# A two-layer decoder trunk on one core: the first column group of the input projection by row-tile halves, with its weights in a space of their own

## The reference

```python
for l in range(DEPTH):                      # 2
    a = rms_norm(h, norm_mix_pre[l])
    mix = hybrid_mixer(a, ...)              # proj = a @ w_in, three kinds of heads, then w_out
    h = h + rms_norm(mix, norm_mix_post[l])
    a = rms_norm(h, norm_x_pre[l])
    h = h + rms_norm(cross_attention(a, rms_norm(mem, norm_mem[l]), ...), norm_x_post[l])
    a = rms_norm(h, norm_ffn_pre[l])
    h = h + rms_norm(conv_ffn(a, ...), norm_ffn_post[l])
return h
```

## Time and profile before

| | |
|---|---|
| Median of three timed runs | 1779.3 us (1778.06 to 1780.26) |
| Profiled execution, its own time | 1777.65 us |
| Its span, first to last instruction | 1775.9 us |
| TensorE busy | 1714.9 us (97%) |
| ScalarE, VectorE, GpSimd busy | 714.2, 667.5, 808.5 us |
| Moved by DMA | 154.15 MB, 87 GB/s |

### The profile page before, as it was taken

The page is one execution under the profiler, slowest core; times in us unless marked ns, Lnnn a source line. Parts: engine busy times, 40 slices in busy tenths (PEclk is TensorE's granted clock), DMA queues, the critical chain, the costliest instruction groups (busy, mean ns, idle before and its releaser), DMA issues.

```text
span 1775.9 us, 23057 instructions
## 1 busy us (share of the span) xinstructions
PE 1714.9 (97%) x9214; PEld 1384.6 (78%) x9214; DVE 667.5 (38%) x1392; ACT 714.2 (40%) x1344; POOL 808.5 (46%) x495
## 2 busy tenths in 40 slices
PE   5999999999999999999989999999999999999997
PEld 4888766788688888888878886768877888888785
DVE  3253566251443223311253446651532622232113
ACT  5325657362453222232253257662633612222222
POOL 4446656364143444445344466563531344443552
PEclk9999989999999999999999999999999999999999
DMA  4324111133122222232232340111421233232321
GB/s 168 107 87 145 49 25 25 60 118 131 36 95 72 95 95 95 86 104 96 96 110 85 106 132 25 25 49 60 155 95 36 72 102 103 98 100 72 119 95 48
DMA packets 100694, 154.15 MB, mean 87 GB/s; under 512 B 4284, under 2 KB 76268, under 8 KB 100588
## 3 DMA queue, kind: packets, MB, share of 16 engines
q1 hardware_dynamic: 97532, 147.16, 25.4%
q10 hardware_dynamic: 3056, 5.51, 1.0%
HBM read 150.56 MB, written 2.10 MB: 86 GB/s over the span
## 4 chain that ended last, share of the span: by engine, by line
PE 89%; DVE 3%; ACT 3%; POOL 2%; issue 1%; DMA 1%; POOLq 0%; ACTq 0%; DVEq 0%
PE banks L1412 24%; PE banks L1414 24%; PE banks L1413 24%; PE banks L1664 4%; PE banks L1642 4%; PE banks L1621 4%; POOL w_lo L686 2%; PE banks L1794 1%; PE banks L1776 1%; ACT w_hi L773 1%; PE banks L1432 1%; PE banks L1614 1%; DVE banks L1112 1%; DVE h L1113 1%; DMA pos_i<-in_positions 1%
## 5 line engine op out<-in xcount | busy, mean ns | idle before, releaser
L686 POOL TENSOR_TENSOR w_lo<-raw,w_hi 128x1024 fp32r<-128x1024 f32 (+2 forms) x272 | 654.2, 2426 | 783.7 <-ACT w_hi L773 783.7
L773 ACT ACTIVATE w_hi<-raw 128x1024 fp32r<-128x1024 f32 (+2 forms) x272 | 267.6, 1028 | 753.2 <-PE banks L1414 740.0
L1412 PE MATMUL banks<-w_hi,a_lo 128*128 128x512 f32 (+1 forms) x928 | 359.4, 387 | 5.8 <-POOL w_lo L686 5.7
L1414 PE MATMUL banks<-w_hi,a_hi 128*128 128x512 f32 (+1 forms) x928 | 355.3, 383 | 0.0
L1413 PE MATMUL banks<-w_lo,a_hi 128*128 128x512 f32 (+1 forms) x928 | 355.2, 383 | 0.0
L1412 PE MATMUL banks<-a_hi,w_lo 128*128 128x512 f32 x768 | 299.6, 390 | 0.0
L1414 PE MATMUL banks<-a_hi,w_hi 128*128 128x512 f32 x768 | 298.8, 389 | 0.0
L1413 PE MATMUL banks<-a_lo,w_hi 128*128 128x512 f32 x768 | 298.8, 389 | 0.0
L1412 PEld LDWEIGHTS banks<-w_hi,a_lo 128*128 128x128 f32 x928 | 174.3, 188 | 44.2 <-POOL w_lo L686 9.2
L1414 PEld LDWEIGHTS banks<-w_hi,a_hi 128*128 128x128 f32 x928 | 174.3, 188 | 33.9
L1413 PEld LDWEIGHTS banks<-w_lo,a_hi 128*128 128x128 f32 x928 | 174.4, 188 | 33.2 <-issue 0.5
(11 more groups left out here) (220 smaller groups left out, 2223.0 us busy)
## 6 DMA issues: line engine op xcount, KB each, us to landing
raw<-in_ffn_w_up SPq DMA_DIRECT2D x44, 1024.0 KB, 5.1
raw<-in_w_in SPq DMA_DIRECT2D x20, 1024.0 KB, 5.0
raw<-in_ffn_w_down SPq DMA_DIRECT2D x20, 1024.0 KB, 4.9
raw<-in_x_wk SPq DMA_DIRECT2D x8, 1024.0 KB, 5.2
raw<-in_x_wv SPq DMA_DIRECT2D x8, 1024.0 KB, 4.9
raw<-in_x_wq SPq DMA_DIRECT2D x8, 1024.0 KB, 5.1
raw<-in_x_wo SPq DMA_DIRECT2D x8, 1024.0 KB, 4.9
raw<-in_cmp_wk SPq DMA_DIRECT2D x4, 1024.0 KB, 5.3
```

The costliest lines, as they stand in the source:

```text
L686: inc(pool.tensor_tensor(lo_flat(u)[:, at], raw_flat(u)[:, at], hi_flat(u)[:, at].bitcast(F32), ALU.subtract), lo_made)
L773: inc(act.activation(hi_flat(u)[:, at], raw_flat(u)[:, at], ACT.Copy), hi_made)
L1412: pe.matmul(dst, st_lo, mv_hi, start=first, stop=False)
L1414: return pe.matmul(dst, st_hi, mv_hi, start=False, stop=last)
```

## The change

1. **Halves.** Group 0 of the input projection is taken out of the loop over c and runs over halves of the row tiles: tiles 0 and 1 with units 0 and 1, then tiles 2 and 3 with the same units. Its activations are made by `transpose_piece`, `hi_pieces` and `lo_pieces`, 16 half-width pieces instead of 8 whole ones. The pieces of the first half go to banks 2 to 5, those of the second to 4 to 7.
2. **Weights of their own.** The splits of units 0 and 1 stand in `proj_r`, a part of the space of `proj` (in the feed-forward stage, of `gT`). Their casts no longer wait for the ring, but for the last split of `gT` (`g_lo`). Layer 1's are cast before the first and before the third `post_sum` of layer 0's closing norm.
3. **Last norm behind.** `post_sum(2, 3)` and `add_post(2, 3)` of layer 0 move into layer 1, behind high pieces 0 to 3 and behind low pieces 0 to 7.
4. **Start.** `x` is loaded in halves: tiles 0 and 1 first, tiles 2 and 3 behind weight units 0 and 1. The four norm vectors of layer 0 are loaded from ScalarE's queue, which issues the positions after them; the four others follow GpSimd's first memset on SyncE's. The angles are made on VectorE behind low piece 7, their sines and the two table loads on ScalarE behind high piece 15.
5. **Memory.** The load of `mem` is issued behind high piece 15.
6. **End.** `h` is stored tile by tile.

```diff
@@ sync
-            sp.dma_start(h[:], x[0].rearrange("(t p) d -> p t d", p=P)).then_inc(pro_x, 16)
-            sp.wait_ge(pro_pool, 5)
+            sp.dma_start(h[:, 0:2], x_tiles[:, 0:2]).then_inc(pro_x, 16)
+            sp.wait_ge(pro_pool, 1)
+            load_vecs(sp, 0, False, True)
+            for u in range(2):
+                sp.dma_start(shape_unit(raw[:, u % RING, :], u), unit_source(0, u)).then_inc(raw_landed[u % RING], 16)
+            sp.dma_start(h[:, 2:4], x_tiles[:, 2:4]).then_inc(pro_x2, 16)
...
-            sp.wait_ge(h_done.sem, h_done.at(DEPTH, 0))
-            sp.dma_start(out[0].rearrange("(t p) d -> p t d", p=P), h[:]).then_inc(stored, 16)
-            sp.wait_ge(stored, 16)
+            for t in range(T):
+                sp.wait_ge(h_done.sem, h_done.at(DEPTH, t - T + 1))
+                sp.dma_start(out[0, P * t:P * t + P, :], h[:, t, :]).then_inc(stored, 16)
+            sp.wait_ge(stored, 16 * T)
@@ shared helpers
+        def half_of(buf, ups, low, u, half):
+            n = unit_width(u) // 2
+            if u < 2 and ups is not None:
+                return proj_r[:, 2 * u + half, 512:2560].rearrange("p (k q n) -> p k q n", q=2, n=512)[:, :, low]
+            flat = whole(u, buf, ups)[:, n * half:n * half + n] if ups is not None else buf[:, u % RING, n * half:n * half + n]
+            return flat.rearrange("p (k n) -> p k n", n=512) if u < 2 else flat
...
+def piece_bank(inst, p):
+    return p % 4 if inst else (2, 4)[p // KD] + p % 4
@@ scalar
+            act.preload_act_table_set("natural_log_exp_and_others")
+            act.wait_ge(pro_pool, 1)
+            load_vecs(act, 0, True, False)
             act.dma_start(pos_i[:, 0:4], ...)
...
-            act.wait_ge(pro_rope, 1)
-            act.activation(sin_t[:].rearrange("p a b -> p (a b)"), ang[:, 0, :], ACT.Sin).then_inc(pro_act, 1)
-            act.activation(cos_t[:].rearrange("p a b -> p (a b)"), ang[:, 1, :], ACT.Sin).then_inc(pro_act, 1)
+            def tables():
+                act.wait_ge(pro_rope, 1)
+                act.activation(sin_t[:].rearrange("p a b -> p (a b)"), ang[:, 0, :], ACT.Sin).then_inc(pro_act, 1)
+                act.activation(cos_t[:].rearrange("p a b -> p (a b)"), ang[:, 1, :], ACT.Sin).then_inc(pro_act, 1)
+                act.wait_ge(pro_act, 2)
+                act.preload_act_table_set("natural_log_exp_and_others")
...
-                            if not U_UP <= u < U_UP + 2:
+                            if not U_UP <= u < U_UP + 2 and u >= 2:
                                 act.wait_ge(unit_used.sem, at_l * UNITS + place_free(u))
+                            if u < 2 and at_l:
+                                act.wait_ge(g_lo.sem, g_lo.at(at_l - 1, 12))
...
+                if l == 0:
+                    cast_halves(1)
                 for i, n in enumerate((64, 88)):
                     act.wait_ge(vecs_T.sem, vecs_T.at(l, i + 1))
...
-                act.wait_ge(h_done.sem, h_done.at(l, 0))
-                act.dma_start(mem_rows[:], ...)
-                hi_parts(0, 0)
+                hi_pieces(0, range(4))
+                if l:
+                    post_sum(2, 3, l - 1)
+                else:
+                    cast_halves(2)
+                hi_pieces(0, range(4, KD))
+                cast_to(2)
+                hi_pieces(0, range(KD, 2 * KD))
+                act.wait_ge(h_done.sem, h_done.at(l, 0))
+                act.dma_start(mem_rows[:], ...)
+                if l == 0:
+                    tables()
+                    act.wait_ge(pro_x, 16)
+                    act.wait_ge(pro_x2, 16)
                 for t in range(T):
                     rms_estimate(h[:, t, :], rows[:, t, :], t, pre_est)
...
-                post_and_pre(2, None)
+                cast_to(UNITS + 1)
+                post_sum(2, 0)
+                post_sum(2, 1)
+                cast_to(UNITS + 2)
+                post_sum(2, 2)
+                if l == DEPTH - 1:
+                    post_sum(2, 3)
@@ vector
-                lo_parts(0, 0)
+                lo_pieces(0, range(KD))
+                if l:
+                    add_post(2, 3, gain_row_ffn, l - 1)
+                else:
+                    tables()
+                lo_pieces(0, range(KD, 2 * KD))
@@ tensor
+                for half in range(2):
+                    if half:
+                        pe.wait_ge(h_done.sem, h_done.at(l, 0))
+                        if l == 0:
+                            pe.wait_ge(pro_x2, 16)
+                        for p in range(KD, KD + 4):
+                            transpose_piece(0, p)
+                    for kh in range(2):
+                        unit(kh)
+                        for t in (2 * half, 2 * half + 1):
+                            st = slice(P * t, P * t + P)
+                            for k in range(4):
+                                a = 4 * kh + k
+                                if t == 2 * half:
+                                    if k == 2:
+                                        rest(kh)
+                                    pe.wait_ge(aT_lo.sem, aT_lo.at(l, KD * half + a + 1))
+                                    if kh == 0:
+                                        transpose_piece(0, KD * half + k + 4)
+                                ins = three(bank(t), a_hi[:, a, st], a_lo[:, a, st], first_piece(kh, k, 0), first_piece(kh, k, 1), a == 0, a == KD - 1)
...
-                for c in range(6):
+                for c in range(1, 6):
```

More of the change, by code:

```diff
@@ new lines, in split_unit, with first_piece @@
+        def split_unit(u):
+            return shape_unit(whole(u, w_hi, up_hi), u), shape_unit(whole(u, w_lo, up_lo), u)
+        def first_piece(u, k, low):
+            return proj_r[:, 2 * u + k // 2, 512 + 1024 * (k % 2) + 512 * low:1024 + 1024 * (k % 2) + 512 * low]
+        def half_of(buf, ups, low, u, half):
[4 more added lines that the diff above has]
+            return flat.rearrange("p (k n) -> p k n", n=512) if u < 2 else flat
@@ L958, in _ @@
                 cast_to(U_XQ + 1)
-                hi_parts(1, 8, range(4))
+                hi_parts(range(4))
                 for b in range(4):
@@ L1400, in _ @@
                     g_rest(i)
-                post_and_pre(2, None, gain_row_ffn)
+                dve.wait_ge(gain_landed[2].sem, gain_landed[2].at(l, 16))
+                for t in range(T if l == DEPTH - 1 else T - 1):
+                    add_post(2, t, gain_row_ffn)
                 dve.sem_clear(dve_chain)
@@ L1419, in unit, with transpose_rows, transpose_piece @@
                     pe.wait_ge(lo_made.sem, lo_made.at(l, 2 * u + 1))
-                    return shape_unit(hi_flat(u), u), shape_unit(lo_flat(u), u)
+                    return split_unit(u)
                 def rest(u):
                     pe.wait_ge(lo_made.sem, lo_made.at(l, 2 * u + 2))
-                def transpose_rows(inst, k):
+                def transpose_rows(k):
                     if k >= 4:
-                        pe.wait_ge(aT_lo.sem, aT_lo.at(l, KD * inst + k - 3))
-                    src = (h, rows)[inst]
+                        pe.wait_ge(aT_lo.sem, aT_lo.at(l, ROWS_AT[1] + k - 3))
                     for t in range(T):
-                        ins = pe.transpose(bank(aT_bank(inst, k), P, P * t), src[:, t, P * k:P * k + P], ident[:])
+                        ins = pe.transpose(bank(4 + k % 4, P, P * t), rows[:, t, P * k:P * k + P], ident[:])
+                    inc(ins, aT_psum)
+                def transpose_piece(inst, p):
+                    half, k = divmod(p, KD)
+                    if inst == 0 and piece_bank(0, p) >= 4:
+                        pe.wait_ge(h_done.sem, h_done.at(l, -1 if piece_bank(0, p) < 6 else 0))
+                    if p >= 4:
+                        pe.wait_ge(aT_lo.sem, aT_lo.at(l, ROWS_AT[inst] + p - 3))
+                    for i in range(2):
+                        ins = pe.transpose(row_piece_psum(inst, p)[:, P * i:P * i + P], (rows if inst else h)[:, 2 * half + i, P * k:P * k + P], ident[:])
                     inc(ins, aT_psum)
@@ L1811, in _ @@
                 rows_gemm(U_XO, 4, 1, lambda i: pe.wait_ge(xo_lo.sem, xo_lo.at(l, 2 * i + 2)), xo_bank)
-                def transpose_piece(p):
-                    half, k = divmod(p, KD)
-                    if p >= 4:
-                        pe.wait_ge(aT_lo.sem, aT_lo.at(l, 2 * KD + p - 3))
-                    for i in range(2):
-                        ins = pe.transpose(row_piece_psum(p)[:, P * i:P * i + P], rows[:, 2 * half + i, P * k:P * k + P], ident[:])
-                    inc(ins, aT_psum)
                 for half in range(2):
```

217 lines of the change are left out of this document (111 added, 106 removed).

## The result

The changed kernel takes **1787.25 us** in the median of eight runs (1782.38 to 1788.51), the kernel before 1778.96 (1778.06 to 1784.48). The ratio is 1.0034, with an interval of 1.0019 to 1.0050, so the change costs 3.4 to 8.9 us, some 6.0. Ten more runs (experiment 5) give 1.0021 (1.0002 to 1.0040), some 3.7 us. The median is inside the predicted range (1776.5 to 1787.5), but by 0.25 us alone, 5.2 us above the predicted 1782.0, and slower by 0.2 to 0.3% where the likeliest forecast was no change that counts.

A forecast was written before the change was run, and what follows sets the result against it. TensorE almost never stands, so only its few stops and the span's two ends could give time back. Terms -5.5, +9.7, -4.9, +7.0 and -3.6 gave +2.7 us: 1780.4 profiled, 1782.0 median, range 1776.5 to 1787.5.

The forecast's parts named there:

- Start of layer 0: First column group of layer 0: unit 0 lands at 9.7, the group ends at 41.6 instead of 47.1, -5.5 us.
- Stop in layer 0: After layer 0's first group, TensorE waits for unit 2's low half, with `tables` also in ScalarE's queue: +9.7 us.
- Change of layer: Layer 1's first group starts without tile 3's norm and ends at 917.6 instead of 922.5: -4.9 us.
- Stop in layer 1: After layer 1's first group, TensorE waits for unit 2's low half: 6.8 us late plus 0.2 for the clock, +7.0.
- Store: Kernel's end: three tiles go out while the last is made, whose 512 KB take 3.0 us instead of 6.6: -3.6.
- What is late next: After group 0 in both layers: unit 2's cast, behind piece 15 and six sums, stops TensorE; +9.7 and +7.0 us.
- Rival 2: The gaps close and nothing opens, unit 2's split being ready in time: -14.0 us, 1765.3; chance 0.10.
- Rival 1: Start: unit 0 lands late, at 12.1, sharing DMA engines: 2.4 us less gain, sum +5.1, 1784.4; chance 0.22.
- rival 4: Change of layer isn't filled (first half waits for tile 3, or casts come late): sum +7.6, 1786.9; chance 0.08.
- At nothing: the weights' new place in `proj_r`: Splits of units 0 and 1 in `proj_r` cost nothing: same element counts, and `gT`'s last split precedes the cast.
- I add 0.2 for the clock: Behind layer 1's stop: 0.2 us added to the 6.8 us lateness for the granted clock.
- slower: Whole kernel over 0.2%, 3.6 us, slower than before: chance 0.42, against 0.44 within and 0.14 faster.

The follow-up runs named there:

- experiment 5: The changed kernel run once more, unaltered: 1787.18 us, ratio 1.0021 to the kernel before.
- experiment 1: The changed kernel with unit 2 cast on ScalarE before high pieces 8 to 15, in both layers: 1767.59 us, ratio 0.9921 to the kernel before.
- experiment 2: The changed kernel with unit 2 cast before high pieces 8 to 15 in layer 1 only: 1777.54 us, ratio 0.9979 to the kernel before.
- experiment 6: The changed kernel with the second half of `x` issued before the weight units: 1789.06 us, ratio 1.0035 to the kernel before.
- experiment 7: The changed kernel with layer 0's splits of units 0 and 1 in the ring instead of in `proj`'s space: 1783.14 us, a single execution.
- experiment 4: The kernel before with only the change's four 512 KB stores instead of one of 2 MB: 1779.96 us, ratio 0.9981.
- experiment 9: The changed kernel with unit 2 cast early in both layers, and high parts apart from low ones in `proj_r`: 1769.6 us, ratio 0.9939 to the kernel before.

## Why the prediction was right and wrong

The third column is the first trace against that of before, the fourth is the trace of experiment 5, the same kernel in a run near the median, against the same trace of before; each is made as under "Where the time went". The trace of before is of a short run (1777.65), so the third column compares like with like, and the fourth shows what a longer run adds.

| Term | predicted | first trace | second trace |
|---|---|---|---|
| Start of layer 0 | -5.5 | -4.9 | -4.1 |
| Stop in layer 0 | +9.7 | +10.1 | +10.5 |
| Change of layer | -4.9 | -4.3 | -4.3 |
| Stop in layer 1 | +7.0 | +6.7 | +8.2 |
| Store | -3.6 | -4.0 | -4.0 |
| Sum | +2.7 | +3.7 | +6.3 |

- **What is late next: right.** This was the step said to decide. The waits were expected at about 8 and 5 us and are 8.06 and 5.02, the squares run unbroken from piece 15 to the cast, and experiments 1 and 2 take the stops away by this one call. Behind layer 1's stop TensorE takes 2.8 us for two k while the second low half is made, as worked out. Rival 2 (nothing opens) was priced at 1765.3 and is not what the change does; experiment 1 made it, and took 1767.6.
- **Start: right in its times.** Unit 0 was expected at 9.7 and is cast at 9.61; the first weight matmul is at 13.51, for 13.35; the first half waits 0.55 and 0.66 us, for 0.6 and 1.0. Rival 1 (12.1) fell, and experiment 6 shows that its price was a little low: 2.4 forecast, against 2.4 at the cast, 3.1 at the group's end and 3.2 in the lowest runs. One reading was off and cost nothing: `tables` was put at 18.8 to 22 on VectorE and took from 18.76 to 26.6, since GpSimd worked beside it.
- **Change of layer: right.** TensorE waits 0.76 us and goes on with the weights at 897.5, 2.2 us behind the boundary as predicted, so rival 4 fell. The norm of tile 3 ends at 904.75, 9.4 us behind the boundary (10.2 were predicted), under the first half.
- **Store: right**, 0.4 undersized. The span ends 3.0 us after the last addition, as said; before it was 7.0. The fixed 2.0 us that the prediction set beside this term (Trainium skill, DMA: Bandwidth & Descriptors, "Anatomy of one DMA") are given there for DMAs of GpSimd's queue, and this store is SyncE's: its 512 KB landed 2.6 us after the issue, of which 1.3 are bytes at 410 GB/s.
- **"At nothing: the weights' new place in `proj_r`": wrong.** Element counts were compared and the matmul's pitch was not asked about. It is 0.5 us a layer (by the pitch in experiment 7), and so most of the 0.6 by which the start and the change of layer each fell short in the first trace. It is a small part of the result, since ScalarE's time ends the stops whatever the pitch is.
- **"I add 0.2 for the clock": mis-sized for a typical run.** The 0.2 was added in layer 1 alone (6.8 and 2.9 are the 9.7 of layer 0). The prediction had the bound (a clock that stays low adds 1.4 a layer) and put none of it in the sum. Behind the stop in layer 1 the first trace loses 6.7 - 5.0 = 1.7 us besides the wait, which agrees; the second loses 8.2 - 5.0 = 3.2, with the lower level for 5.9 us. The difference of 1.5 is about the 1.4 of the bound. With 0.4 more in layer 0 and 0.7 at the start, by the pitch, the sum becomes +6.3. The ratios say +6.0 and +3.7, the lowest runs +4.3 and +4.5. How much of the medians' distance is this clock and how much the attention stages is not shown, since the kernel before has no trace of a long run.
- **The attention stages** were left out of the sum as untouched. They are, but in layer 1 the stage took 250.0 us before, 251.7 in the first trace, 253.3 in the second and 257.6 in experiment 4, and the mean granted clock from 1040 to 1240 fell in the same order: 0.98, 0.96, 0.95, 0.94. What lowers the clock there is not shown. Whether a stop upstream makes such dips likelier is not shown: the kernel before has runs at 1784 to 1788 too, and experiment 4, without the change's stops, has the longest stage of these.

The forecast's sum of +2.7 stood 0.9 under the bound of 3.6 at which "slower" begins, with 1.4 a layer known and left out of it. With both it was +5.5, and more of the chance should have gone to "slower", which had 0.42. That the median of 1787.25 still lies in the range is luck: its upper end was set by the first rival, which fell, and nothing in the sum stands for the spread of the attention stages.

## What to carry to other kernels

When a block is made finer and starts earlier, look on each in-order engine for what stood behind its last piece: here six sums of squares and a weight cast lost the 19 us that had covered them, and one call moved ahead of the second half turned a loss of 4 to 6 us into a gain of 11 to 14. Price a stop of TensorE as the wait and what the lower clock takes behind it, here 1.7 to 3.2 us a stop, and take it from several runs, not from one trace. Ask of a tile that is moved in SBUF not only who waits for the space, but also whether its reader runs at the same pitch.

## What the runs showed of the hardware that was not expected

**The clock behind a stop.** With the same code and waits of the same length, the lower level lasted 2.8 to 2.9 us in three traces and 5.9 to 6.0 in two after the stop in layer 1; after layer 0's stop it was 3.6 to 4.8 us. The Trainium skill, TensorE: Matmul & The Clock Gate, "What's actually happening", calls the slow stretch at a kernel's start variable from run to run, and behind these stops the traces show the same; it also puts the ramp under 1% of a usual kernel, which holds here (1.7 to 3.2 of 1780 us a stop) and yet is of the size of what this change costs.

**Small VectorE operations beside GpSimd.** Eight operations of 128x5 elements took 0.67 us before, when GpSimd stood still (at 11.30). After, GpSimd was making two low halves (19.35 to 24.13), and they ended with it:

```profile
18.96 5.20 DVE L1138 TENSOR_SCALAR ang<-pos_f 128x5 f32<-128x5 f32 x8
```

```profile
19.35 4.78 POOL L721 TENSOR_TENSOR proj_r<-raw,proj_r 128x1024 fp32r<-128x1024 f32 x2 [3.45 <-ACT proj_r L814]
```

They cost nothing there: the next low piece comes at 29.39 and waits for ScalarE. In experiment 1 they cost 1.35 us of TensorE's time (the rows there): a copy of 128x40, 0.18 us without GpSimd, takes 2.33, and the operation behind it 2.31, until GpSimd has made both low halves of unit 2, at 29.9. The low pieces, which VectorE reads out of PSUM, aren't held: 0.48 us each beside GpSimd or not. The Trainium skill, GPSIMD Engine Reference, "8. Key points", says that the two engines share their interfaces to SBUF and contend for some forms of VectorE's instructions; these rows agree, and show a small operation of VectorE waiting for as long as one of GpSimd's lasts.

**The place of the moving operand.** Read out of `proj_r` a 512-column matmul follows after 0.232 us, whichever way the pieces are laid out there, and out of the ring at the same place of group 0 after 0.227 (experiments 7 and 9). The place is not all: behind layer 1's stop, from 931.39 to 933.70, matmuls out of the ring follow after 0.231 too, and after 0.227 later on.
